# A hybrid block with a mixture of 32 experts: from blocks of 64 tokens on 64-column tiles to blocks of 32 tokens on 32-column tiles, with 16 KB and 8 KB weight rows and the output in PSUM

## The reference

```python
def _moe(h, router_w, router_b, w_gate_up, b_gate_up, w_down, b_down):
    logits = (hf @ router_w + router_b).astype(jnp.float32)
    top_val, top_idx = lax.top_k(logits, TOP_K)                  # 4 of 32
    probs = jax.nn.softmax(top_val, axis=-1)
    combine = jnp.sum(jax.nn.one_hot(top_idx, N_EXPERTS) * probs[..., None], axis=1)
    for e in range(N_EXPERTS):
        gu = hf @ w_gate_up[e] + b_gate_up[e]                    # 1024 x 2048
        g, lin = gu[:, :D_EXPERT], gu[:, D_EXPERT:]
        g = jnp.minimum(g, SWIGLU_LIMIT)
        lin = jnp.clip(lin, -SWIGLU_LIMIT, SWIGLU_LIMIT)
        act = g * jax.nn.sigmoid(SWIGLU_ALPHA * g) * (lin + 1.0)
        out = out + combine[:, e:e + 1] * (act @ w_down[e] + b_down[e])   # 1024 x 1024
```

## Time and profile before

| | |
|---|---|
| median of 3 runs | 1250.24 us (1249.51 to 1250.9) |
| the profiled execution | 1253.29 us, with a span of 1251.5 us |
| PE, PEld, DVE, ACT, POOL busy | 92%, 42%, 26%, 15%, 4% of the span |
| DMA | 436.44 MB; 349 GB/s over the span, 415 to 417 GB/s in most of the loop |
| mean granted TensorE clock | 0.988 |
| loop over the blocks | from 252.9 us to 1236.9 us |

### The profile page before, as it was taken

The page is one execution under the profiler, slowest core; times in us unless marked ns, Lnnn a source line. Parts: engine busy times, 40 slices in busy tenths (PEclk is TensorE's granted clock), DMA queues, the critical chain, the costliest instruction groups (busy, mean ns, idle before and its releaser), DMA issues.

```text
span 1251.5 us, 18998 instructions
## 1 busy us (share of the span) xinstructions
PE 1150.6 (92%) x7144; PEld 526.0 (42%) x7145; DVE 324.3 (26%) x761; ACT 186.8 (15%) x274; POOL 48.1 (4%) x43
## 2 busy tenths in 40 slices
PE   6999999699999998889999988888888999998895
PEld 5877886443334333333334333333333334333332
DVE  7799152711121111111121111111111112111113
ACT  1311230311111111111111111111111111110002
POOL 1002140200000000000000000000000000000001
PEclk9999999799999999999999999999999999999998
DMA  9462564784999999998999999999999899999992
GB/s 267 159 182 98 185 247 170 271 318 186 352 415 415 415 417 415 416 415 361 364 415 415 416 415 417 415 416 415 415 415 417 323 393 415 416 415 416 414 417 105
DMA packets 117303, 436.44 MB, mean 349 GB/s; under 512 B 17713, under 2 KB 34161, under 8 KB 96705
## 3 DMA queue, kind: packets, MB, share of 16 engines
q1 hardware_dynamic: 117152, 436.05, 88.5%
q10 hardware_dynamic: 128, 0.08, 0.0%
HBM read 432.72 MB, written 1.05 MB: 347 GB/s over the span
## 4 chain that ended last, share of the span: by engine, by line
PE 47%; SPq 27%; DMA 12%; DVE 9%; issue 4%; ACT 1%; ACTq 0%; DVEq 0%
PE ps L1457 18%; SPq L456 14%; DMA ring<-in_w_gate_up 12%; PE ps L1466 11%; SPq L446 8%; PE ps L1195 7%; SPq L449 5%; PE ps L1331 2%; PE ps L1379 2%; PE ps L1418 1%; DVE rD L1130 1%; DVE rD L1133 1%; DVE rD L1126 1%; PE ps L1281 1%; PE ps L1343 1%
## 5 line engine op out<-in xcount | busy, mean ns | idle before, releaser
L1457 PE MATMUL ps<-ring,rD 128*64 128x512 f32 x1808 | 414.5, 599 | 48.3 <-DMA ring<-in_w_gate_up 48.0
L1457 PEld LDWEIGHTS ps<-ring,rD 128*64 128x64 f32 x1808 | 124.0, 137 | 327.6 <-issue 189.9
L1466 PE MATMUL ps<-ring,rD 128*64 128x512 f32 x1120 | 248.1, 595 | 4.5 <-issue 4.5
L1126 DVE TENSOR_SCALAR rD<-ps 128x512 f32<-128x512 f32 x35 | 24.2, 692 | 472.0 <-PE ps L1457 472.0
L1466 PEld LDWEIGHTS ps<-ring,rD 128*64 128x64 f32 x1120 | 80.0, 137 | 145.5 <-issue 144.0
L1195 PE MATMUL ps<-ring 128*128 128x256 f32 (+1 forms) x448 | 105.0, 395 | 1.7 <-DVE ring L810 1.7
L705 ACT ACTIVATE rD<-rD 128x512 f32<-128x512 f32 x35 | 22.0, 630 | 536.1 <-DVE rD L1126 536.1
L1195 PEld LDWEIGHTS ps<-ring 128*128 128x128 f32 x448 | 86.4, 195 | 18.0 <-issue 3.4
L1057 DVE CAST rE<-rE 128x64 bf16 (+1 forms) x36 | 7.0, 196 | 299.5 <-PE ps L1457 299.5
L1427 PE MATMUL ps<-rD,rE 64*128 64x512 f32 x288 | 71.5, 615 | 0.7 <-ACT rD L711 0.7
L1418 PEld LDWEIGHTS ps<-rE,rC 128*128 128x128 bf16 x1728 | 58.5, 99 | 27.0 <-issue 26.5
(11 more groups left out here) (332 smaller groups left out, 759.3 us busy)
## 6 DMA issues: line engine op xcount, KB each, us to landing
ring<-in_w_gate_up SPq DMA_DIRECT2D x160, 1024.0 KB, 17.6
ring<-in_w_down SPq DMA_DIRECT2D x256, 512.0 KB, 18.3
ring<-in_w_gate_up SPq DMA_DIRECT2D x96, 512.0 KB, 15.1
ring<-in_w_in SPq DMA_DIRECT2D x14, 1024.0 KB, 6.1
rC<-in_w_gate_up SPq DMA_DIRECT2D x16, 512.0 KB, 15.6
rF<-in_w_gate_up SPq DMA_DIRECT2D x16, 512.0 KB, 15.1
rU<-in_w_gate_up SPq DMA_DIRECT2D x16, 512.0 KB, 15.0
rQ<-in_w_gate_up SPq DMA_DIRECT2D x16, 512.0 KB, 15.3
```

The source lines that it names most:

```text
L1126: nc.vector.tensor_scalar(g1, ps[:, 0, :], LIMIT, None, ALU.min).then_inc(g1_ready, 1)
L1457: ins = nc.tensor.matmul(ps[64 * h:64 * h + 64, a, :], xT[:, k, :], gsl[odd][k][a][:, h, :], start=False, stop=(k == KT - 1), skip_group_c ...
L1466: ins = nc.tensor.matmul(ps[64 * h:64 * h + 64, 2, :], actT[:, k % 4, 64 * (k // 4):64 * (k // 4) + 64], dsl[odd][k][:, h, :], start=(k == ...
```

## The change

Blocks have BS = 32 tokens. By the counts above there are then 46: 3 for experts 1 and 23, 4 for expert 10, 2 for experts 11, 12, 15, 18, 19, 26 and 30, and 1 for each of the other 22. Every column half of 512 becomes four quarters of QW = 256, on the four 32-column tiles. The 128x512 operands of DVE and ACT are 128x256. The moving operand of the gather has 32 columns.

A load of w_gate_up brings PAIR = 2 slices, n = 0 to 3, in rows of 16 KB (the slice k is now made of rows k, k + 8, k + 16, ...; the second norm writes its result permuted to match). A load of w_down brings rows of 8 KB. The first AHEAD = 2 pairs of odd experts lie in `late` and `early`, the old buffers joined. An expert's groups are A = pairs 2 and 3, B = 4 loads of w_down, C = pairs 0 and 1.

The output lies in PSUM by column quarters, a bank for each (4 + q), and the residual is put there by 8 identity matmuls ahead of the routing, where 4 matmuls cleared the banks. So the end adds nothing: ACT squares out of PSUM and DVE multiplies by the gain out of PSUM, half by half, the table for the square root is loaded beforehand, and DVE and ACT each scale one of the two halves of the tokens. `gfin` is loaded after the last weights. POOL has no part in it.

```diff
-BS = 64
+BS = 32
+NQ = P // BS
+QW = D // NQ
-NBC = NBLK + 1
-AHEAD = 3
-TURNS = 5
+NBC = NBLK + 2
+PAIR = 2
+NPAIR = KT // PAIR
+AHEAD = 2
+TURNS = 4
...
+        def gu_rows(e, n):
+            rows = T["w_gate_up"][0, e].rearrange("o (p k) n -> p (o k) n", k=KT)
+            return rows[:, PAIR * n:PAIR * n + PAIR, :].rearrange("p k n -> p (k n)")
+        def dn_rows(e, q):
+            rows = T["w_down"][0, e].rearrange("o (q p j) n -> p (o q) (j n)", q=NQ, j=2)
+            return rows[:, q, :]
...
+                for n in range(first, until):
+                    sp.wait_ge(gu_done, last * KT + PAIR * (n + 1))
+                    sp.dma_start(gsl[odd][n], gu_rows(bass.ds(e, 1), n)).then_inc(gu_in[odd][n], 16)
...
+                for q in range(NQ):
+                    sp.wait_ge(dn_done, last * KT + 2 * (q + 1))
+                    sp.dma_start(dsl[odd][q], dn_rows(bass.ds(e, 1), q)).then_inc(dn_in[odd][q], 16)
...
-            pe.wait_ge(late_consts, 7)
-            for b in range(4, 8):
-                nc.tensor.matmul(ps[:, b, :], ebias[:, 0, :], upper.unsqueeze(1).to_broadcast([P, 4, P]), start=True,
-                                 stop=False, skip_group_check=True)
-
+            def residual(c):
+                for q in range(NQ):
+                    nc.tensor.matmul(ps[:, 4 + q, S * c:S * c + QW], ident[:, :], h2[:, c, QW * q:QW * q + QW], start=(c == 0),
+                                     stop=False, skip_group_check=True)
...
             def scatter(last=False):
                 for c in range(ST):
-                    for h in range(2):
-                        ins = nc.tensor.matmul(ps[:, 4 + 2 * c + h, :], selT[64 * h:64 * h + 64, c * P:(c + 1) * P],
-                                               ysb[64 * h:64 * h + 64, :], start=False, stop=False,
-                                               skip_group_check=True, tile_position=(64 * h, 0))
+                    for q in range(NQ):
+                        ins = nc.tensor.matmul(ps[:, 4 + q, S * c:S * c + QW],
+                                               selT[BS * q:BS * q + BS, c * P:(c + 1) * P], ysb[BS * q:BS * q + BS, :],
+                                               start=False, stop=False, skip_group_check=True, tile_position=(BS * q, 0))
...
                     for a in range(2):
-                        for h in range(2):
-                            ins = nc.tensor.matmul(ps[64 * h:64 * h + 64, a, :], xT[:, k, :], gsl[odd][k][a][:, h, :],
+                        for q in range(NQ):
+                            at = (k % PAIR) * SLOT + a * D + QW * q
+                            ins = nc.tensor.matmul(ps[BS * q:BS * q + BS, a, 0:QW], xT[:, k, :], gsl[odd][n][:, at:at + QW],
                                                    start=False, stop=(k == KT - 1), skip_group_check=True,
-                                                   tile_position=(0, 64 * h))
+                                                   tile_position=(0, BS * q))
...
-            for c in range(ST):
-                for h in range(2):
-                    dve.wait_ge(scattered, 2 * c + h + 1)
-                    part = h2[:, c, 512 * h:512 * h + 512]
-                    link(TT(part, part, ps[:, 4 + 2 * c + h, :], ALU.add))
+            dve.wait_ge(scattered, 1)
+            dve.wait_ge(fin_in, 16)
+            for h in (1, 0):
+                if h == 0:
+                    dve.wait_ge(sumsq, 4)
+                for c in range(ST):
+                    ins = TT(hr[:, c, 512 * h:512 * h + 512].rearrange("p (q n) -> p q n", n=QW),
+                             ps[:, 4 + 2 * h:6 + 2 * h, S * c:S * c + QW],
+                             gfin[:, 512 * h:512 * h + 512].rearrange("p (q n) -> p q n", n=QW), ALU.mult)
```

More of the change, by code:

```diff
@@ L157, in build @@
         gffn = view(rF, 0, D)
-        gfin = view(rF, D, D)
+        gfin = view(ring, KT * SLOT, D)
         rw = view(rU, 0, KT, EXP)
@@ L194, in build @@
-        cmp = view(rE, 1744, NBC, rows=EXP)
-        off = view(rE, 1792, NBC)
-        v8 = view(rE, 1840, ST, 8)
-        rs1 = view(rE, 1856, 16)
-        cur = view(rE, 1872, 4)
+        g1 = view(rD, 0, QW)
+        l1 = view(rD, QW, QW)
+        sg = view(rD, 2 * QW, QW)
+        actT = view(rD, 3 * QW, 2, P)
+        ysb = view(rD, 2048, QW)
+        xT = view(rD, 2048 + QW, KT, BS)
+        upper = view(rP, MT * CW - P, P, dt=BF16)
+        onesb = view(rP, MT * CW - P // 2, P, dt=BF16)
@@ new lines, in build @@
+        slots = view(rE, 1792, NQ, BS)
+        blks = view(rE, 1920, NBC)
+        tri = view(rE, 1988, EXP, rows=EXP)
+        cur = view(rE, 2024, 4)
+        onehot = view(rE, 0, ST, BS, dt=BF16)
+        wsel = view(rE, 32, ST, P)
+        selT = view(rE, 288, S)
+        ebias = view(rE, 544, BS, dt=BF16)
+        blkcol = view(rE, 560, 4, NBC)
+        bk = view(rE, 820, NBC)
+        lg = view(rE, 888, ST, EXP)
+        gt = view(rE, 952, ST, EXP)
+        eq = view(rE, 1016, ST, EXP)
+        ce = view(rE, 1080, ST, EXP)
@@ L199, in build @@
+        mask = view(rE, 1144, ST, EXP)
+        ex = view(rE, 1208, ST, EXP)
+        posm = view(rE, 1272, ST, EXP)
+        maskb = view(rE, 1336, ST, EXP, dt=BF16)
+        cmp = view(rE, 1368, NBC, rows=EXP)
+        off = view(rE, 1436, NBC)
+        comb = view(rE, 1504, ST, NQ, EXP)
+        v8 = view(rE, 1760, ST, 8)
+        rs1 = view(rE, 1776, 16)
         pcT = view(rQ, 0, 4, P, rows=EXP)
@@ L210, in build @@
         pmod = sb("pmod", [P, 1])
-        rT = sb("rT", [P, 1024])
         es = view(rT, 0, NB, NPH)
@@ L467, in _ @@
             last = used_by(EXP - 4)
-            load_gu(EXP - 3, 1, AHEAD, KT, last)
+            load_gu(EXP - 3, 1, AHEAD, NPAIR, last)
             load_dn(EXP - 2, 0, last)
@@ L1477, in one_block @@
                 for a in range(2):
[L1478 to L1481 removed]
+                    for q in range(NQ):
+                        nc.tensor.matmul(ps[BS * q:BS * q + BS, a, 0:QW], ebias[0:96, :],
+                                         bp[:, a * D + QW * q:a * D + QW * q + QW], start=True, stop=False,
+                                         skip_group_check=True, tile_position=(0, BS * q))
                 pe.wait_ge(xT_ready, i + 1)
@@ L1495, in one_block @@
                 pe.wait_ge(act_ready, i + 1)
-                for j in range(4):
-                    ins = nc.tensor.transpose(ps[:, 0, j * P:(j + 1) * P], l1[:, j * P:(j + 1) * P], ident[:, :])
+                for j in range(2):
+                    ins = nc.tensor.transpose(ps[:, 0, j * P:(j + 1) * P], g1[:, j * P:(j + 1) * P], ident[:, :])
                 ins.then_inc(act_tr, 1)
```

281 lines of the change are left out of this document (124 added, 157 removed).

## The result

The changed kernel takes 1260.09 us (median of 4, 1258.69 to 1260.59), the kernel before in the same session 1249.88 us (1248.48 to 1250.9). The ratio is 1.0081, with a 95% interval of 1.0063 to 1.0098: slower, by some 10 us. The forecast was 1242 us, faster.

A forecast was written before the change was run, and what follows sets the result against it. It took PE and the weight transfer to bound the kernel alternately. 254 + 906.4 transfer + 62.4 gaps + 7 clock + 1.2 last down + 11.5 end gave a span of 1242.5, forecast as 1242 us, range 1228 to 1262.

The forecast's parts named there:

- The rate: Weight loads: 16 KB rows move at 427.5 GB/s, 8 KB rows at 422, so 385.9 MB take 906.4 us, 22.6 less.
- The pitch rule: Loads of w_gate_up: 16 KiB copies slow down at large power-of-two row pitches, 207 GB/s at 512 KiB; a possible slowdown.
- Packing and block count: PE's blocks: matmuls run four abreast at 56.1 ns each, in 46 blocks; gate and up 7.3 us, down 3.6.
- rival 1: PE's matmuls: four tiles abreast don't pack as in the first part; block up to 16.9 us, total 1277; chance 0.08.
- The block as a whole: One 32-token block on PE, from bias to down, was to take 14.8 us, between 14.4 and 16.9.
- The gaps: Loads stopped while group A waits for its places, at the start and experts 1, 10, 23, 30: 62.4 us together.
- the formula: Stop at an expert of m blocks: A's release after (m - 1) x 14.8 us, less 19.75 of B and C, plus restart.
- What a microsecond of the block is worth: Each us of longer block on PE was to cost the whole kernel some 15 us.
- The bound that I gave for being wrong: PE's block: the forecast counts as wrong if a block takes over 15.4 us, where the time of before is reached.
- The clock: PE at half clock after pauses delays releases at experts of several blocks: 0 to 19 us, taken as 7.
- Rival 2: PE's half clock costs its full 19 us, giving 1254 us, slower than before; chance 0.17.
- The end: From the last down through scatter, norm and store: 11.5 us, between 10.5 and the 14.6 of before.

The follow-up runs named there:

- oldrows: Changed kernel with each load of a pair split in two DMAs of the old row sizes, 8 KB of w_gate_up and 4 KB of w_down: 1280.46 us.
- Short_block: Changed kernel with 6 of 8 slices of w_down multiplied in down, the last two only loaded: 1242.6 us.
- one_block: Changed kernel with at most one block for each expert, tokens beyond its first 32 left out: 1185.52 us.
- Fewer_turns: Changed kernel with 4 turns in place of 8 in the second loop of PE, ACT and DVE: 1257.49 us.
- b64: Changed kernel with its blocks kept at 64 tokens on 64-column tiles (35 blocks): 1240.13 us, ratio 0.9911 to the kernel before.

## Why the prediction was wrong

- **The rate: right.** 425 to 428 GB/s where 427.5 was worked out, and oldrows shows that the row size makes it. The 386 MB took about 905 us, forecast 906.4. The pitch rule of the Trainium skill, DMA: Bandwidth & Descriptors, section Latency and other measured facts, has its figures from a pitch of 512 KiB on. At the 64 KiB of this kernel no slowing shows, with 425 to 428 GB/s.
- **Packing and block count: right.** The bias took 0.25 us (forecast 0.3), gate and up 7.05 (7.3), down 3.66 (3.6), and there are 46 blocks; rival 1 falls. The DVE chain, 597.17 - 595.06 = 2.11 us, was 2.03. Transposes and half gather took 1.18 instead of 1.57.
- **The block as a whole: too short.** 15.33 us instead of 14.8. The term that I hadn't is 1.08 us for the two value loads, which the kernel before hid: its idle time ahead of the bias is nil, and ahead of down 0.24. I had read the 1.10 us between the earlier trace rows's gather and down as all that a branch costs, and taken it over. The transposes and half gather were forecast 0.39 us too long, and gate and up with the bias 0.30, which hid more than half of the missing term. With all these lengths right the forecast would have been 14.25 us; that 14.8 came so near is in part luck.
- **The gaps: this is the step that failed.** The prediction put 62.4 us for them, with 7 more for the clock. Lost by windows of 1 us: start 4.3 (2), expert 1 21.2 (13.5), expert 10 30.2 (27.1), expert 23 17.1 (12.3), expert 30 10.3 (7.5), experts 11 and 12 2.3 (0): 85.4, which is 16.0 over the two terms. At expert 10 the formula can be read off: from the last landing to the release 608.95 - 561.54 = 47.4 us (44.4), from the landing to the stop about 18.8 (19.75), from the release to the traffic 1.2 (2.5). Its form was right, the block's 0.5 us goes in three times, and half clock in the first block adds 1.2. At expert 1 the stall of 4.50 us and another of 1.01 (at 258.79 us, in the first block's gate and up) come on top; the prediction had no such term, and what makes the stall stays open. Whoever forecasts a stop as a difference of two sums of 20 to 47 us has an error of 1 us in one of them in full.
- **What a microsecond of the block is worth: near, by luck.** The prediction said some 15 us. Short_block got 17.5 for 1.0, of which some 5.7 are the vanished stall at expert 1 and the clock behind it, so the length by itself is worth about 12. The bound that I gave for being wrong, a block over 15.4 us, was too far out: at 15.33 the time was already 10 us over that of before, for the 0.5 us of the block explain only 6 to 8 of the 18 us that were missing.
- **The clock: about right.** From the last landing's matmuls to the end of down it took 9.9 us at expert 10, 10.6 at 23 and 10.3 at 30, against 8.65 where PE runs on: 4.8 us, and 2.4 at expert 1, for the 7 that I took. The mean granted clock was 0.91. At single blocks half speed costs nothing, which one_block shows. Rival 2's 19 us aren't there.
- **The end: 3.8 us too short.** 15.3 us from the last down instead of 11.5. From the scatter on it is 11.6, where 11.1 was worked out. What was missing is the exit over four unused turns, 3.7 us where ACT's copy was to take 0.4. Fewer_turns shows it. That the kernel before hid its exit under a down of 7.09 us is my reading; its scatter waits 0.7 us, for ACT.
- **The sum.** +16.0 for the gaps, +3.8 for the end, -1.3 for a start at 252.7 instead of 254, -1 for the rate: 17.5 us, where the span is 16.3 over the forecast of 1242.5; 1.2 us of this don't add up.
- **The question that wasn't asked** is what the parts do apart. The rows and the new end bring 10 us (b64; the end 0.7 of them), the blocks take 20. Of the rate's 22.6 us, b64 already loses 10 to stops that pairs make longer. PE's busy time fell from 1150.6 to 973.3 us on the pages, and that bought nothing: at one block an expert it was hidden under the transfer, and at three or four it was the number of blocks that counted: 14.3 us for each block behind the second.
